# The dots read the current chunk's tokens from PSUM; projections and transposes share banks with the mixers

## The reference

```python
def reference(x, ...):
    for l in range(DEPTH):                       # 2
        h = _rms(x, g_mix_norm[l])
        x = x + _mixer_block(h, w_in[l], ...)    # 11 input projections of 256 columns, 4 mixers, w_out
        h = _rms(x, g_ffn_norm[l])
        x = x + _peer(h, w_peer_q[l], peer_sub_keys[l], peer_u[l], peer_v[l])

def chunk(xc):                                   # _peer, 128 tokens at a time
    q = (xc @ w_q).reshape(C, PEER_HEADS, 2, PEER_HALF)          # 8 heads, 2 halves of 128
    s = jnp.einsum('thpd,hpkd->thpk', q, sub_keys)
    sv, si = lax.top_k(s, PEER_TOPK)                             # 16 of 128 keys a half
    ...                                                          # best 16 of the 256 pairs: eidx
    g = jax.nn.softmax(top, axis=-1)
    a = jnp.einsum('thkd,td->thk', u_tab[eidx], xc)              # 128 dots of 1024 a token
    w = g * jax.nn.gelu(a)
    return jnp.einsum('thk,thkd->td', w, v_tab[eidx])
```

## Time and profile before

| | |
|---|---|
| three timed runs | 3364.05, 3382.74, 3389.28 us (median 3382.74) |
| span of the profiled execution, first to last instruction | 3383.4 us |
| its own time beyond the span | not printed; the span stands 0.7 us above the median |
| instructions | 27538 |
| moved by DMA | 1205.57 MB, 356 GB/s over the span |
| first gather issued at | 140.7 us |

### The profile page before, as it was taken

One profiled execution on the slowest core, in us unless ns is written; L12 is line 12 of the kernel. 1 busy time (PEld: TensorE's weight loads), 2 busy tenths in 40 slices (PEclk: granted clock), 3 DMA queues, 4 the chain that ended last, 5 costly groups with the idle time before them and its releaser, 6 DMA issues.

```text
span 3383.4 us, 27538 instructions
## 1 busy us (share of the span) xinstructions
PE 2560.1 (76%) x7696; PEld 1422.5 (42%) x7696; DVE 2327.2 (69%) x5442; ACT 690.9 (20%) x1655; POOL 2291.7 (68%) x2052
## 2 busy tenths in 40 slices
PE   6568777986777778877787787987787778666667
PEld 5545344743443435533353443643354334222222
DVE  2495678568689875666668886666668888655554
ACT  2112212123311111112211221123322122101011
POOL 0156766566667676676776777677777777777776
PEclk9789888988888888998899998998899899888888
DMA  5489999998899999998999999999999999999998
GB/s 235 174 320 406 358 377 371 343 378 310 308 376 367 347 344 407 401 379 332 352 394 369 379 373 348 390 397 344 348 358 397 363 382 368 368 367 359 366 366 336
DMA packets 316375, 1205.57 MB, mean 356 GB/s; under 512 B 37184, under 2 KB 37440, under 8 KB 301248
## 3 DMA queue, kind: packets, MB, share of 16 engines
q0 software_dynamic: 294912, 1073.87, 83.9%
q1 hardware_dynamic: 21312, 129.94, 9.7%
HBM read 1201.57 MB, written 2.10 MB: 356 GB/s over the span
## 4 chain that ended last, share of the span: by engine, by line
PE 30%; POOL 22%; issue 18%; DVE 17%; DMA 7%; ACT 3%; another core or an unknown queue 2%; SPq 0%; DVEq 0%; ACTq 0%; POOLq 0%
POOL ring L479 22%; PE psY L815 15%; PE psP L694 8%; DMA ring<-in_v,idx 6%; DVE ring L1067 5%; PE psP L689 4%; DVE x L1076 1%; DMA ring<-in_u,idx 1%; DVE sc L860 1%; PE psT L675 1%; ACT diag L656 1%; DVE hot L1031 1%; DVE hot L1032 1%; DVE pick L1033 1%
## 5 line engine op out<-in xcount | busy, mean ns | idle before, releaser
L815 PE MATMUL psY<-ring,diag 128*128 128x512 f32 x3120 | 1689.6, 685 | 678.0 <-DMA ring<-in_v,idx 270.3
L479 POOL DMA_INDIRECT ring<-in_u,idx x1024 | 1148.1, 1121 | 588.1 <-issue 304.3
L1067 DVE CUSTOM_DVE_ANT_0 ring<-ring,htok 128x1024 f32<-128x1024 f32 x1024 | 1232.4, 1223 | 450.5 <-DMA ring<-in_u,idx 396.5
L479 POOL DMA_INDIRECT ring<-in_v,idx x1024 | 1143.3, 1117 | 490.2 <-issue 284.2
L815 PEld LDWEIGHTS psY<-ring,diag 128*128 128x128 f32 x3120 | 636.9, 216 | 1545.9 <-issue 1087.1
L656 ACT ACTIVATE diag<-cst,wgt 128x128 f32<-128x128 f32 x780 | 275.5, 393 | 480.8 <-PE psY L815 184.9
L1076 DVE SCALAR_TENSOR_TENSOR x<-ring,wgt,x 128x1024 f32<-128x1024 f32 x244 | 313.6, 1285 | 39.5 <-DMA ring<-in_v,idx 27.6
L694 PE MATMUL psP<-wr,hT 128*128 128x256 f32 x1392 | 312.7, 383 | 5.1 <-DMA wr<-in_w_out 3.0
L689 PE MATMUL psP<-hT,wr 128*128 128x256 f32 (+1 forms) x1664 | 314.8, 350 | 0.7 <-ACT hT L517 0.7
L689 PEld LDWEIGHTS psP<-hT,wr 128*128 128x128 f32 x1664 | 282.2, 200 | 49.7 <-issue 23.1
L694 PEld LDWEIGHTS psP<-wr,hT 128*128 128x128 f32 x1392 | 267.6, 193 | 65.4 <-issue 22.9
(11 more groups left out here) (125 smaller groups left out, 1652.3 us busy)
## 6 DMA issues: line engine op xcount, KB each, us to landing
wr<-in_w_in SPq DMA_DIRECT2D x44, 1024.0 KB
wr<-in_w_q SPq DMA_DIRECT2D x40, 1024.0 KB
wr<-in_w_out SPq DMA_DIRECT2D x19, 1024.0 KB
ring<-in_u,idx POOLq DMA_INDIRECT x1024
ring<-in_v,idx POOLq DMA_INDIRECT x1024
ring<-in_w_in SPq DMA_DIRECT2D x11, 1024.0 KB, 13.2
x<-in_x SPq DMA_DIRECT2D x4, 512.0 KB, 20.1
sub<-in_subkeys SPq DMA_DIRECT2D x2, 1024.0 KB
```

What stands on the lines that cost most here:

```text
L479: pool.indirect_dma_start(out=ring[:, q % NB], out_offset=None, in_=table, in_offset=bass.IndirectOffsetOnAxis(ap=idx[:, s % NS, n:n + 1], ...
L815: last = nc.tensor.matmul(psY[:, b * 512:(b + 1) * 512], diag[:, m % ND], r[:, b * 512:(b + 1) * 512], start=first, stop=final)
L1067: v.tensor_tensor_reduce(out=r, in0=r, in1=htok[:, s % NS], scale=1.0, scalar=0.0, op0=ALU.mult, op1=ALU.add, accum_out=adot[:, n:n + 1]). ...
```

## The change

- `psP` and `psT` keep one bank each; a new tensor `psH` takes the two banks that come free.
- ACT copies the current step's tokens from htok into psH (`place_h`): once before the first head and then at the end of each step, after all its dots and before the gelu of its last head. DVE's first dot of a step waits for it (`h_placed`). The dots read psH instead of htok.
- Projection pieces with an odd number write into psO, those with an even one into psP. psO's order of users (`PSO_USERS`) now has the odd pieces and the mixers' outputs in one list.
- Of the wide parts' two batches of transposes, the first goes to psT and the second to psS, whose list of users (`PSS_LIST`) now has the wide parts; "dil T" and "conv" all go to the one psT.
- The 19 blank lines at the head of the file are gone, so the lines of the profile after are smaller at first.

```diff
-PSS_LIST = list(numbers("pe", "scores", "logits", "key scores"))
+WIDE = ("hT1", "qk", "catT", "hT2")
+PSS_LIST = list(numbers("pe", "scores", "logits", "key scores", *WIDE))
+PSO_USERS = [k for k in numbers("pe", "dil out", "sgu", "sums", "stick out", "piece")
+             if (k[0] != "dil out" or k[2] == 0) and (k[0] != "piece" or PIECE_NO[k[1], k[2]] % 2)]
...
-for _part, _s, _i in numbers("pe", "hT1", "qk", "dil T", "conv", "catT", "hT2"):
+for _part, _s, _i in numbers("pe", "dil T", "conv", *WIDE):
     BATCH_NO[_part, _s, _i] = _batches
-    _batches += 1 if _part in ("dil T", "conv") else 2
+    IN_PST.append(_batches)
+    _batches += 2 if _part in WIDE else 1
...
         psY = ps("psY", [P, D])
-        psP = ps("psP", [P, 2, 512])
-        psT = ps("psT", [P, 2, 512])
+        psH = ps("psH", [P, D])
+        psP = ps("psP", [P, 512])
+        psT = ps("psT", [P, 512])
...
+        def piece_bank(G):
+
+            return psO if G % 2 else psP
+
+        def batch_bank(b):
+
+            return psT if b in IN_PST else psS
+
+        def pso_free_for(part, s, i):
+
+            n = PSO_USERS.index((part, s, i))
+            if n == 0:
+                return None
+            before = PSO_USERS[n - 1]
+            if before[0] == "piece":
+                return psp_freed(PIECE_NO[before[1:]])
+            return pso_free, PSO_NO[before] + 1
...
+            if part in WIDE:
+                return tp_taken, BATCH_NO[part, s, i] + 2
...
+            def place_h(s):
+
+                act.wait_ge(normed, NORMED_NO["norm2", s] + 1)
+                if s:
+                    act.wait_ge(dotted, SLOTS * s)
+                nc.scalar.activation(psH[:], htok[:, s % NS], ACT.Copy).then_inc(h_placed, 1)
...
+            place_h(0)
             for J in range(HEADS + 1):
...
                     act.wait_ge(dotted, TOPK * (J + 1))
                     if J:
                         act.wait_ge(w_ready, J)
+                    if (J + 1) % PH == 0 and J + 1 < HEADS:
+                        place_h((J + 1) // PH)
...
             def transposes(b, srcs):
 
-                if b >= 2:
-                    pe.wait_ge(tp_taken, b - 1)
...
+            def wait_pst(b):
+
+                n = IN_PST.index(b)
+                if n:
+                    pe.wait_ge(tp_taken, IN_PST[n - 1] + 1)
+
+            def wide_transposes(part, s):
+
+                b = BATCH_NO[part, s, 0]
+                wait_pst(b)
+                transposes(b, [hn[:, k * P:(k + 1) * P] for k in range(4)])
+                wait_for(pe, pss_free(part, s, 0))
+                transposes(b + 1, [hn[:, k * P:(k + 1) * P] for k in range(4, 8)])
...
-                if G >= 2:
+                if G % 2:
+                    wait_for(pe, pso_free_for("piece", s, i))
+                elif G:
                     pe.wait_ge(*psp_freed(G - 2))
-                bank = psP[:, G % 2]
+                bank = piece_bank(G)
...
             def pso_wait(part, s, i):
-                if PSO_NO[part, s, i]:
-                    pe.wait_ge(pso_free, PSO_NO[part, s, i])
+                wait_for(pe, pso_free_for(part, s, i))
...
+                        if n == 0:
+                            dve.wait_ge(h_placed, s + 1)
                         landed(dve, ("u", J, k))
                         r = ring[:, at[("u", J, k)] % NB]
-                        v.tensor_tensor_reduce(out=r, in0=r, in1=htok[:, s % NS], scale=1.0, scalar=0.0,
+                        v.tensor_tensor_reduce(out=r, in0=r, in1=psH[:], scale=1.0, scalar=0.0,
                                                op0=ALU.mult, op1=ALU.add, accum_out=adot[:, n:n + 1]).then_inc(dotted, 1)
```

More of the change, by code:

```diff
@@ L499, in take_batch @@
                 act.wait_ge(tp_ready, b + 1)
-                nc.scalar.activation(dst, psT[:, b % 2, :width], ACT.Copy).then_inc(tp_taken, 1)
+                nc.scalar.activation(dst, batch_bank(b)[:, :width], ACT.Copy).then_inc(tp_taken, 1)
             def row_sumsq(s):
@@ L517, in take_hT @@
                         last = nc.scalar.activation(hT[:, 4 * b:4 * b + 4, o],
-                                                    psT[:, n % 2].rearrange("p (k t) -> p k t", t=P), ACT.Copy)
+                                                    batch_bank(n)[:].rearrange("p (k t) -> p k t", t=P), ACT.Copy)
                     else:
                         for k in range(4):
-                            last = nc.scalar.activation(hT[:, 4 * b + k, o], psT[:, n % 2, k * P:(k + 1) * P], ACT.Copy,
+                            last = nc.scalar.activation(hT[:, 4 * b + k, o], batch_bank(n)[:, k * P:(k + 1) * P], ACT.Copy,
                                                         scale=gain_t[:, gain, 4 * b + k:4 * b + k + 1])
@@ L541, in front @@
                         act.wait_ge(cat_sq, s)
-                    src = psP[:, G % 2, :n * PW].rearrange("p (j w) -> p j w", j=n)
+                    src = piece_bank(G)[:, :n * PW].rearrange("p (j w) -> p j w", j=n)
                     if i < 4:
@@ L551, in front @@
                     else:
-                        src = psP[:, G % 2, :n * PW].rearrange("p (b j t) -> p b j t", b=2, j=n)
+                        src = piece_bank(G)[:, :n * PW].rearrange("p (b j t) -> p b j t", b=2, j=n)
                         dst = fm[:, i - CB, :, :n]
@@ L628, in front @@
                         act.wait_ge(s_scores, TOP_NO[GROUP_OF[s0][-1], h0] + 1)
-                    nc.scalar.activation(qT[:, Q % 2, :, :n * P], psP[:, G % 2, :n * PW].rearrange("p (b t) -> p b t", b=2),
+                    nc.scalar.activation(qT[:, Q % 2, :, :n * P], piece_bank(G)[:, :n * PW].rearrange("p (b t) -> p b t", b=2),
                                          ACT.Copy).then_inc(psp_act, 1)
@@ L670, in transposes @@
             def transposes(b, srcs):
-                if b >= 2:
-                    pe.wait_ge(tp_taken, b - 1)
                 for i, src in enumerate(srcs):
-                    last = nc.tensor.transpose(psT[:, b % 2, i * P:(i + 1) * P], src, ident)
+                    last = nc.tensor.transpose(batch_bank(b)[:, i * P:(i + 1) * P], src, ident)
                 last.then_inc(tp_ready, 1)
+            def wait_pst(b):
[8 more added lines that the diff above has]
+                transposes(b + 1, [hn[:, k * P:(k + 1) * P] for k in range(4, 8)])
             def project(s, i):
@@ L734, in front @@
                     pe.wait_ge(normed, n + 1)
-                    for b in range(2):
-                        transposes(BATCH_NO[part, s, 0] + b, [hn[:, (4 * b + k) * P:(4 * b + k + 1) * P] for k in range(4)])
+                    wide_transposes(part, s)
                 elif part == "piece":
@@ L743, in front @@
                     pe.wait_ge(qk_done, s + 1)
-                    for b in range(2):
-                        transposes(BATCH_NO["qk", s, 0] + b, [hn[:, (4 * b + k) * P:(4 * b + k + 1) * P] for k in range(4)])
+                    wide_transposes("qk", s)
                 elif part == "scores":
@@ L749, in front @@
                     pe.wait_ge(weighed, H * s + i + 1)
+                    wait_pst(BATCH_NO["dil T", s, i])
                     transposes(BATCH_NO["dil T", s, i], [prob[:, i % 2, b * P:(b + 1) * P] for b in range(c + 1)])
@@ L998, in front @@
                     xs = x[:, c:c + n, i * PW:(i + 1) * PW]
-                    v.tensor_tensor(xs, xs, psP[:, G % 2, :n * PW].rearrange("p (j w) -> p j w", j=n),
+                    v.tensor_tensor(xs, xs, piece_bank(G)[:, :n * PW].rearrange("p (j w) -> p j w", j=n),
                                     ALU.add).then_inc(psp_dve, 1)
```

6 lines of the change are left out of this document (4 added, 2 removed).

## The result

The kernel after takes 3439.77 us (median of 5 runs, 3433.09 to 3455.05) against 3382.74 of the kernel before (5 runs, 3364.05 to 3389.28): ratio 1.018, 95% interval 1.0147 to 1.0213. It is slower by 57 us where 98 us less were forecast. The profiled execution took 3455.05 us; its span is 3453.2.

A forecast was written before the change was run, and what follows sets the result against it. No single bound: POOL late in the run, PE and DVE where the next chunks' mixers are squeezed in. 3383.4 - 108 (POOL) + 10 (copies) + 5 (banks) = 3290, less 5 for PE's clock: 3285 us, range 3165 to 3365.

The forecast's parts named there:

- the mean gather: POOL's gathers: mean time to fall from 1.12 to 0.97-1.00 us, median unchanged.
- Banks and copy together: Costs on the path: +10 us for 8 copies into PSUM, +5 us for hand-overs of the shared banks.
- Rival C: Hand-overs at 35 changes of tenant in psO and psS stop PE's in-order queue: 3466 us; chance 0.05.
- The mean rate: DMA over the whole span: to rise from 356 to 366 GB/s.
- PE's waits at psO and psS: PE's waits for the shared banks: to stay under 20 us in all.
- rival B: Nothing passes: POOL's excess is hidden behind transfers, or contention has another cause; only costs remain, 3398 us; chance 0.09.
- 291 us of POOL time go: POOL's 364 us of gather excess: 0.8 of it released by moving the dots' operand; bounds 255 and 364.
- The 0.8 for the dots' share: Share of POOL's gather excess due to dots: 70% of counted two-SBUF-operand DVE time, taken as 0.8.
- the 13 us for the "issue" entry: The chain's 18% "issue": POOL's excess, 4% of some 400 us there, adds 13 us of gain.
- What is that worth?: POOL on the chain: 291 us released x 0.326 takes 95 us out of the path that set the end.
- what is late next: the data itself: Late part: gathers issued every 1.24 us would need 421 GB/s, best seen 418, so landing takes over from POOL.
- The DMA bound: Skill's HBM limit of some 358 GB/s per core would make the gain zero; stretches at 406 to 418 spoke against it.

The follow-up runs named there:

- a_htok: The changed kernel with the dots reading htok in SBUF again, all else kept: 3271.45 us, 1.0014 of the kernel before.
- a_again: The changed kernel unedited, run again on a chip where the kernel before takes 3270.94 us: 3213.48 us, ratio 0.9826.
- a_htok2: The changed kernel with the dots on htok in SBUF again, where the kernel before takes 3351.35 us: 3357.12 us, 1.0011 of before.
- a_third: The changed kernel unedited, run again on a chip where the kernel before takes 3351.35 us: 3438.05 us, ratio 1.0245.
- The small pad: The changed kernel with a 128x16 memset and a wait for it on POOL ahead of every gather; where before takes 3351.35 us: 3462.46 us, 1.0354 of before.
- the limit of 7: The changed kernel with at most 7 gathers in flight, where the kernel before takes 3351.35 us: 3453.06 us, 1.0302 of before.
- x_reduce: The changed kernel with each dot replaced by a sum over the gathered row alone, one SBUF operand and no PSUM: 3208.28 us, 0.9849 of before.
- batch 3: Runs sent together on one chip, where the kernel before takes 3351.35 us and the changed kernel 3438.05 us, ratio 1.0245.
- a_fourth: The changed kernel unedited, run again on a chip where the kernel before takes 3262.10 us: 3212.47 us, ratio 0.9854.

## Why the prediction was wrong

*Right, and by its own steps.* No engine's work grew; the dot's time (-6 ns, forecast -8); a gather under a dot at 0.94; the mean gather at 1.004 us, at the edge of 0.97 to 1.00; POOL's waits for DVE and PE growing from 330 us (to 624); the copy at 1.03 us. Banks and copy together: +15 forecast, and some +4 measured in each of two batches, which can't be told from nothing. Rival C (hand-overs) fell with a_htok, though the result lies near its 3466 us.

*Signs that missed.* The mean rate was to rise to 366 GB/s; it is 349 here and 375 in a_again. PE's waits at psO and psS were to stay under 20 us; they were 57 in before already and are 74. DVE was to idle 1 to 2.5 us at each of the 8 copies, and did so at one (0, 0.3 or 5.7 at the others). By its sign (the gather's time falls, the kernel's doesn't) the result is rival B's, but not by its reason: the gathers weren't hidden behind full transfers, since the rate fell.

*A size that was off.* The term "291 us of POOL time go" measured 235 (203 and 231 in the other pairs). The 0.8 for the dots' share was about right: by the DVE instruction under which each gather of before starts, dots hold 309 of 372 us of excess (over 0.937 us each). What the sum left out is that the gathers then start under other instructions: L1076 held 33 us of excess in before, and as L1108 it holds 115 in after. (In the 13 us for the "issue" entry, 4% of 400 would be 16; nothing hangs on it.)

*The step that failed.* "What is that worth?": 95 us taken from the path, with "what is late next: the data itself". On the chips where before takes 3262 to 3271 us this step holds in kind: the release gave 48 to 57 us by the timed runs, 0.24 to 0.28 of it where 0.326 was taken; with 203 in place of 291 and that factor it would have said 66. On the result's chip the thing late next was not the data but word of it: POOL came to its ring waits 235 us earlier in sum, and updates of semaphores, already late at times in before, came late three times as often on DVE's chain (112 against 34). POOL's waits took 304 us. Neither the forecast nor a rival had this, and the range ended at 3365. That the late updates are what brought these waits is the likeliest reading, and not shown.

The trace of before had signs of it, in rows that the prediction used, and it passed them over. A program of one core has no other core, yet its chain has "another core or an unknown queue 2%", a DVE instruction stood 7.45 us for "remote", and POOL had 19.4 us of it. The chain by engine in a_htok, then in a_htok2, the same kernel on the two kinds of chip:

```profile
PE 27%; POOL 22%; DVE 12%; DMA 11%; issue 9%; ACT 2%; ACTq 0%; DVEq 0%; POOLq 0%
```

```profile
PE 26%; POOL 24%; issue 13%; DVE 10%; DMA 6%; ACT 2%; another core or an unknown queue 1%; DVEq 0%; ACTq 0%; POOLq 0%
```

Only the second has that entry and the larger share of "issue". The forecast took "issue" for POOL's own gaps and added 13 us of gain for them; part of it was waits whose end wasn't recorded, as this trace lacks two in five of the updates.

*What stays open.* That late updates cost time is shown at single places (the 1.87 and 4.15 us above). That they cause the loss as a whole is argued from the account of POOL's waits, which goes with them over the traces; no run takes them away. Why a chip has them, and whether the dots' reads of PSUM or gathers issued in long undisturbed runs make them more frequent, is open. The length of such a run isn't all of it. Of the recorded updates of DVE's chain that came when POOL had issued 12 or more gathers with pauses of at most 0.35 us, 36 of 72 were late in after and 29 of 73 in a_third, but only 17 of 298 in before and 10 of 411 in a_htok2. The small pad and the limit of 7 left the late updates as they were, and x_reduce, which could have told the two apart, ran only on the kind of chip without them. No version was shown to beat both kernels on both kinds of chip.

## What to carry to other kernels

Before pricing a stall of POOL, see what lies under it on DVE: two operands in SBUF cost a gather nearly what the DVE instruction still had to run (up to 1.03 us under a dot). Moving one of them to PSUM, or needing only one, frees it, and 0.24 to 0.30 of the freed time reached the end here. Price as well what the freed instructions will run into next (here L1108). Look first for "remote" in the trace of a one-core program: in these traces it marks updates that arrive late, and where it stood, a gain that rests on one engine reaching its waits sooner turned into a loss. Measure such a change on more than one chip before believing its sign.

## What the runs showed that was not expected

- The same two kernels compare at 0.983 to 0.985 on two chips and at 1.018 and 1.0245 in the result and in batch 3, with intervals of 0.002 to 0.0034 to either side; the kernel before itself differs by 2.4 to 3.7% between the kinds.
- An instruction that waits only for its own engine's last update can start 1.87 us after that one's end, in a stretch at 413 GB/s; on the other kind of chip no update of this chain was later than 0.03 us, though slices of a_fourth, whose chain runs until 2766 us, reach 411 GB/s.
- The rate late in the run: 352 GB/s in a_third, 409 in a_again, over the same 350 us of each (columns as in the earlier trace rows; a_again's line is the second fence):

```profile
2800.00:3150.00 350.00, 227.87 (x492) 98.92 (x492) 226.45 (x506) 50.85 (x137) 223.59 (x230) 0.86 0.93 352
```

```profile
2800.00:3150.00 350.00, 242.40 (x406) 90.48 (x404) 211.36 (x315) 40.49 (x111) 265.88 (x273) 0.83 1.03 409
```

- The DMA bound that the prediction weighed (the Trainium skill, DMA: Bandwidth & Descriptors, section "Where 436 GB/s comes from": some 358 GB/s for a core's HBM) doesn't hold here: a_again moves 375 GB/s over its span.
